# Reading the first kept half of every FFN unit ahead of the preceding unit's last Silu

## The reference

```
def swiglu(h, w_up, w_down):
    gate, up = jnp.split(h @ w_up, 2, axis=-1)      # w_up: 1024 x 5632, 22 tiles of 128 for gate and for up
    return (jax.nn.silu(gate) * up) @ w_down        # w_down: 2816 x 1024
```

## Time and profile before

| | us |
|---|---|
| median of 3 runs | 938.85 (938.18 to 939.34) |
| profiled execution, its own time | 938.98 |
| span from the first to the last instruction | 937.1 |
| TensorE busy | 915.0 (98% of the span) |
| VectorE busy | 674.0 (72%) |
| ScalarE busy | 444.7 (47%) |
| GpSimd busy | 107.9 (12%) |

### The profile page before, as it was taken

One profiled execution on the slowest core, in us unless ns is written; L12 is line 12 of the kernel. 1 busy time (PEld: TensorE's weight loads), 2 busy tenths in 40 slices (PEclk: granted clock), 3 DMA queues, 4 the chain that ended last, 5 costly groups with the idle time before them and its releaser, 6 DMA issues.

```text
span 937.1 us, 22363 instructions
## 1 busy us (share of the span) xinstructions
PE 915.0 (98%) x9385; PEld 887.6 (95%) x9385; DVE 674.0 (72%) x1254; ACT 444.7 (47%) x824; POOL 107.9 (12%) x135
## 2 busy tenths in 40 slices
PE   5999999999999999999999999999999999999997
PEld 4899989998999999999999999999999999999997
DVE  4778879865577677487766888899334999994454
ACT  6687445424234554753223257456213666563223
POOL 0110011112020110100100002122001322220000
PEclk8999999999999999999999999999999999999998
DMA  9834234444333422325643332332323433323312
GB/s 346 273 81 144 60 99 117 125 115 118 112 108 105 130 80 69 102 68 182 186 143 91 91 90 72 87 91 81 92 86 105 113 111 92 92 79 98 89 51 96
DMA packets 146030, 104.80 MB, mean 112 GB/s; under 512 B 5153, under 2 KB 138855, under 8 KB 144779
## 3 DMA queue, kind: packets, MB, share of 16 engines
q1 hardware_dynamic: 138955, 79.16, 29.0%
q0 software_dynamic: 6352, 22.00, 7.8%
q10 hardware_dynamic: 624, 2.23, 0.7%
HBM read 100.06 MB, written 3.31 MB: 110 GB/s over the span
## 4 chain that ended last, share of the span: by engine, by line
PE 91%; ACT 3%; DVE 2%; issue 1%; DMA 1%; SPq 1%; DVEq 0%; ACTq 0%
PE G L2235 60%; PE G L2330 18%; PE R L2243 11%; PE R L2246 1%; DMA wada<-in_w_ada_s 1%; SPq L1120 1%; DVE sum_lo L1780 0%; DVE w_sum L1771 0%; ACT L1291 0%; ACT inp L1291 0%; ACT w_hi L1370 0%; ACT w_hi L1275 0%; DVE cy L1906 0%; DVE cy L1907 0%; DVE cy L1903 0%
## 5 line engine op out<-in xcount | busy, mean ns | idle before, releaser
L2235 PE MATMUL G<-h_hi,w_hi 128*128 128x272 f32 (+1 forms) x880 | 263.4, 299 | 0.2 <-DVE ff_shift L2181 0.2
L2235 PE MATMUL G<-h_lo,w_hi 128*128 128x272 f32 (+1 forms) x880 | 253.9, 289 | 0.0
L2235 PE MATMUL G<-h_hi,w_lo 128*128 128x272 f32 (+1 forms) x880 | 253.6, 288 | 0.0
L1664 DVE TENSOR_TENSOR w_lo<-raw,w_hi 128x1024 fp32r<-128x1024 f32 (+3 forms) x111 | 118.7, 1069 | 82.1 <-ACT w_hi L1275 81.0
L2235 PEld LDWEIGHTS G<-h_hi,w_hi 128*128 128x128 f32 x880 | 165.7, 188 | 3.3 <-DVE ff_shift L2181 0.4
L2235 PEld LDWEIGHTS G<-h_lo,w_hi 128*128 128x128 f32 x880 | 166.0, 189 | 0.3 <-issue 0.3
L2235 PEld LDWEIGHTS G<-h_hi,w_lo 128*128 128x128 f32 x880 | 165.8, 188 | 0.0
L1275 ACT ACTIVATE w_hi<-raw 128x1024 fp32r<-128x1024 f32 (+3 forms) x111 | 101.5, 914 | 113.8 <-PE G L2235 113.5
L2330 PE MATMUL G<-x_hi,sum_hi 128*128 128x272 f32 x288 | 83.7, 291 | 1.1 <-ACT partial L1388 1.1
L2330 PE MATMUL G<-x_hi,sum_lo 128*128 128x272 f32 x288 | 83.4, 290 | 0.0
L2330 PE MATMUL G<-x_lo,sum_hi 128*128 128x272 f32 x288 | 83.0, 288 | 0.0
(11 more groups left out here) (337 smaller groups left out, 2111.4 us busy)
## 6 DMA issues: line engine op xcount, KB each, us to landing
raw<-in_w_in SPq DMA_DIRECT2D x48, 512.0 KB, 4.1
raw<-in_w_up SPq DMA_DIRECT2D x44, 512.0 KB, 4.1
w_ada<-in_w_ada_t POOLq DMA_DIRECT2D x49, 256.0 KB, 3.0
wada<-in_w_ada_s SPq DMA_DIRECT2D x8, 1024.0 KB, 13.4
raw<-in_w_down SPq DMA_DIRECT2D x14, 384.0 KB, 3.4
raw<-in_w_down SPq DMA_DIRECT2D x16, 320.0 KB, 3.1
raw<-in_w_out SPq DMA_DIRECT2D x8, 512.0 KB, 4.0
w_ada_t<-in_w_ada_t POOLq DMA_DIRECT2D x15, 256.0 KB, 3.3
```

The source lines that it names most:

```text
L1664: dve.tensor_tensor(lo, raw[:, i % RAW, 0:job.nk, 0:job.m], hi.bitcast(F32), ALU.subtract).then_inc(w_lo_done, 1)
L2235: ins = pe.matmul(out, w, x, start=(job.first and k == 0 and p == 0), stop=(job.last and k == job.nk - 1 and p == 2))
```

## The change

Read 0 of every unit but the first of a run is now listed ahead of the preceding unit's last Silu, as it was for unit 1 alone. For units 2 to 5 and 7 to 17 it so moves from behind d_hi. Since the read of unit u + 1 may now come while the value of unit u is still to be used, read 0 has two places: `acc` for odd units, the first place of `partial` for even ones. The wait for the place is on the c11 of two units before.

```
             if u == 1:
                 do("q_read", u, 1)
                 do("q_read", u, 2)
-            else:
+            elif u == us[0]:
                 do("q_read", u, 0)
...
-            if nxt == 1:
+            if nxt is not None:
                 do("q_read", nxt, 0)
             do("q_silu", u, 0)
...
         def kept(u, r):
 
-            return acc[:, 0:HALF] if (u, r) == (1, 0) else partial[:, r, :]
+            return acc[:, 0:HALF] if r == 0 and u % 2 else partial[:, r, :]
...
                     act.wait_ge(q_done, 7 * u + READS[r] + 1)
-                    if r == 0 and u == 2:
-                        act.wait_ge(q_out, 3)
-                    elif u and (r or u > 1):
-                        act.wait_ge(q_out, 3 * (u - 1) + (3, 2, 1, 2)[r])
+                    owner = u - (1 if r else 2)
+                    if owner >= 0:
+                        act.wait_ge(q_out, 3 * owner + (3, 2, 1, 2)[r])
                     elif not u:
                         wait_slot(act, groups_before[0] - 1)
```

## The result

The changed kernel takes 949.28 us (median of 4 runs, 947.61 to 950.75), against 938.72 for the kernel before beside it (4 runs, 938.18 to 939.34). The ratio is 1.0111, 95% interval 1.0095 to 1.0127: 1.1% slower, 10.6 us by the medians. The forecast was 948.7.

The account below looks back on a forecast made before the run. TensorE goes at the pace of a ScalarE-VectorE loop that it just touches. Ten units at 0.82 us (8.2) and 1.6 for units 3 and 4 make 9.8 us more, 948.7 by the median; range 942.0 to 952.0.

Parts of the forecast that it names:

- Silu waits for the read in every even unit: ScalarE, units 3, 4, 7 to 16: read 0 waits for the first product's end, so Silu starts 1.05 us later.
- Rival D: c11 comes later than the first product's end, the read costs Silu nothing, the loop shortens: 937.0 us; chance 0.03.
- The queue behind it: ScalarE behind read 0: Silu, d_hi, a_hi, w_hi follow in measured slots, putting read 1 at 749.35.
- P3: Fourth of a unit's seven TensorE products: waits for read 1, 0.39 us late plus 0.09 in its first matmul.
- rival A: GpSimd doesn't hold a_lo, only the fourth product's wait is left: 0.32 us a unit, 942.7 us; chance 0.15.
- the path to P6: VectorE's a_lo, w_lo, add 2, add 4 to the unit's last product: 0.82 us later, setting a period of 11.54.
- a_lo held by GpSimd: GpSimd's add of sum 1 starts before VectorE's a_lo and holds it; add 2 comes 0.82 us later.
- The sum: Units 7 to 16 lose 8.2 us, units 3 and 4 lose 1.6, together 9.8, giving 948.7 us.
- Unit 2 counted at 0: In unit 2 the 0.79 us wait moves from the third product to the fourth; at most 0.2 us gained.
- Rival C: GpSimd's second add gets ahead of VectorE's add 4, last product another 1.35 us late: 25.7 us, 964.5; chance 0.13.

Follow-up runs that it names:

- the run that took it away: Changed kernel with read 1 moved ahead of w_hi, so that the fourth product no longer waits for it: 960.06 us, ratio 1.0209.
- the fill: GpSimd's add of sum 1 replaced by a constant fill, except in a run's first unit: 940.73 us on the changed kernel, 935.61 on the kernel before.
- The run with read 3 first: Kernel before with read 3 moved ahead of the rounding of sum 4 on ScalarE: 937.81 us, ratio 0.9986.
- the read behind Silu: Kernel before with read 0 placed between Silu and d_hi: 944.75 us, ratio 1.0056.

## Why the prediction was right

*Silu waits for the read in every even unit.* Right. After P0's end read 0 waits, and Silu starts 0.29 later (0.30 predicted). c11, 745.73 plus 0.43, ends 0.80 ahead of the read, a margin of 0.75 predicted (from the start of Silu, 0.03 behind c11's end). Rival D needed the opposite.

*The queue behind it.* Right to some hundredths: from read 0 to read 1 it is 2.74 us (749.70 less 746.96), 2.74 predicted.

*P3.* Its last predecessor started at 749.66 and the stream is 0.126 apart, so it is 0.33 late, and its first matmul takes 0.39 where 0.29 is usual: 0.33 and some 0.10, for 0.39 and 0.09 predicted. The read's end releases P3 after 0.04, where I had taken the 0.10 of P6. Without GpSimd's hold it costs 0.45 measured, 0.48 by the terms of rival A. That it lies inside the path to P6, as the prediction has it, is not shown: the run that took it away changed the order at add 4.

*a_lo held by GpSimd.* Right, and this was the choice between ends far apart. It ends 0.58 past GpSimd's end (750.66 against 750.08; 0.60 predicted), and the runs that let a_lo go free, by 0.09 us of order or by the fill, show 0.71 and 0.73. Rival A, which had it free, gave units of 11.04; the fill made them so (11.01). The Trainium skill (SBUF — State Buffer, section "SBUF: two separate sides") states that of the two the one that starts first has the port for its whole instruction, and that a VectorE instruction with two SBUF inputs meets this only against a GpSimd instruction that reads SBUF. The traces agree with both halves: GpSimd 0.27 ahead held a_lo to 1.78, a_lo 0.09 ahead held GpSimd to 1.77, and beside the fill, which reads nothing, a_lo took 0.73.

*The sum.* 10 x 0.82 + 1.6 = 9.8 predicted, 9.8 in the stretch; unit 11.54 predicted, 11.52 measured. That the two sums agree to the tenth is luck in part. From P6 to P6 in the two timelines units 7 to 16 lost 8.0, not 8.2, units 3 and 4 lost 1.55, and units 5 and 17, counted at 0, lost 0.1 and 0.2 at P3, inside the bounds that the prediction gave them.

*Unit 2 counted at 0.* Right, as its rows of after show (the last Silu of unit 1, still released by c11, and P3; beside the earlier trace rows):

```profile
619.68 0.43 ACT L1393 ACTIVATE sq<-sq 128x272 f32<-128x272 f32 x1 [0.59 <-DVE sq L1795]
...
622.57 0.39 PE L2329 MATMUL G<-x_hi,sum_hi 128*128 128x272 f32 x1 [0.89 <-ACT partial L1387]
```

The wait of 0.79 at P2 became one of 0.89 at P3.

*What was imprecise.* Rival D took the loop of before to run through ScalarE's chain alone, so that a shorter chain would free the unit. The run with read 3 first kept 10.72, and only taking GpSimd's add out brought 10.56: the loop runs through that add too. Rival C's margin, 0.14 us by my rows, was 0.12 in after; it held there and gave way as soon as P3 did not wait. By so little was the forecast's order kept. (Rival C's own sum is 26.0 by its terms, not 25.7: 10 x 2.17 and 2 x 12.89 less 21.51.)

The split of 0.80 into 0.45 and 0.35 rests on the fill, which also shortens GpSimd's work to 0.53 us. No run freed a_lo in the changed order with all sums still computed on GpSimd.

## What to carry to other kernels

On an in-order engine, moving an instruction ahead moves its wait ahead as well: before moving a read forward, ask when its producer ends, against when the instruction that it passes would have started (here some 0.8 us later, and with the read's own slot Silu came 1.05 later), and then add up everything queued behind. Where VectorE and GpSimd meet, a delay of tenths of a microsecond changes who goes first, so check each such meeting for its margin, and don't expect that a wait taken away makes the kernel faster. A view of waits shows less than the loss, where instructions overlap in a full stream.

## What was unexpected of the hardware

- Taking away a wait of TensorE (0.18 us shown, 0.45 a unit in cost) made a unit 0.85 us longer, since GpSimd's next add then won by 0.31 us over VectorE's add 4, which took 1.53 us instead of 0.68.
- GpSimd's add of 128x512 took 1.30 us alone and up to 1.77 when it had to wait for a VectorE instruction; in the two cases shown its end came 1.15 to 1.16 us after that instruction's end (after: 750.08 against 748.92, by d_lo; the read behind Silu: 749.76 against 748.61, by a_lo).
- A GpSimd fill of the same tile took 0.53 us and ran beside a_lo with no loss to it (0.73 us).
